# Norm of differential attention's outputs per tile with tokens in the partitions, their turn later and in banks 4 and 5, operand splits inside the last eight tiles' turns

## The reference, cut to what matters

```python
def diff_attention(q, k_sh, v_sh, ...):           # 6 heads of 2 x 64, values 128 wide
    ...
    p = jax.nn.softmax(s, axis=-1)
    attn = (p[:, :, 0] - lam * p[:, :, 1]).astype(v.dtype)
    o = jnp.einsum('bhqk,bkhe->bqhe', attn, v)    # allowed keys end with the query's chunk
    ...
    o = rms_norm_2(o, subln) * (1.0 - lam_init)   # over the 128 values of one head and token
    return o.reshape(B, S, BR_W)

y_mem = memory_cross_attention(q_mem, mem_n, w_mem_kv[l])
y = jnp.concatenate([y_br * jax.nn.silu(gate), y_mem * jax.nn.silu(g_mem)], axis=-1) @ w_out[l]
x = x + rms_norm_2(y, post_norm[l])
```

## Time and profile before

| | us |
|---|---|
| median of 3 runs | 3361.38 (3348.8 to 3362.89) |
| the profiled execution | 3360.08 |
| its span, first to last instruction | 3358.8 |
| stretch of the 48 attention tiles | about 2889 to 3176.4 |
| norm and first splits, no product running | 3176.4 to 3208.4 |
| products with `w_out` | 3208.4 to 3329 |
| last norm, residual and stores | 3329 to 3358.8 |

### The profile page before, as it was taken

One profiled execution on the slowest core, in us unless ns is written; L12 is line 12 of the kernel. 1 busy time (PEld: TensorE's weight loads), 2 busy tenths in 40 slices (PEclk: granted clock), 3 DMA queues, 4 the chain that ended last, 5 costly groups with the idle time before them and its releaser, 6 DMA issues. The chain is left out here.

```text
span 3358.8 us, 49940 instructions
## 1 busy us (share of the span) xinstructions
PE 2869.6 (85%) x20746; PEld 2299.7 (68%) x20746; DVE 1713.3 (51%) x3034; ACT 988.9 (29%) x1803; POOL 688.4 (20%) x531
## 2 busy tenths in 40 slices
PE   7978878799999999689999867777758899998767
PEld 6766666588888888467788546666637678766545
DVE  3425555544444444675554167676644433467534
ACT  3214444311111111633221211121134222244543
POOL 2112233211101110252111022222112211122123
PEclk9988999899999999899999979899979899999978
DMA  3111032011111111122112100000022201010222
GB/s 105 45 50 39 14 101 69 25 57 44 51 50 44 44 57 45 38 79 84 38 39 66 46 1 3 3 3 3 23 93 82 94 20 51 27 38 29 83 77 76
DMA packets 196449, 162.45 MB, mean 48 GB/s; under 512 B 5200, under 2 KB 173818, under 8 KB 195458
## 3 DMA queue, kind: packets, MB, share of 16 engines
q1 hardware_dynamic: 196226, 159.26, 15.1%
HBM read 137.19 MB, written 22.05 MB: 47 GB/s over the span
## 5 line engine op out<-in xcount | busy, mean ns | idle before, releaser
L721 PE MATMUL ps<-r,r 128*128 128x512 f32 (+1 forms) x2304 | 944.0, 410 | 142.4 <-DVE r L686 115.4
L722 PE MATMUL ps<-r,r 128*128 128x512 f32 (+1 forms) x2304 | 914.5, 397 | 0.0
L723 PE MATMUL ps<-r,r 128*128 128x512 f32 (+1 forms) x2304 | 912.8, 396 | 0.0
L721 PEld LDWEIGHTS ps<-r,r 128*128 128x128 f32 x2304 | 446.4, 194 | 274.2 <-DVE r L686 128.9
L667 POOL TENSOR_TENSOR sb<-sb 128x1024 f32<-128x1024 f32 x138 | 280.6, 2039 | 1350.3 <-DMA sb<-in_w_ffn_up 488.6
L723 PEld LDWEIGHTS ps<-r,r 128*128 128x128 f32 x2304 | 445.4, 193 | 95.3
L722 PEld LDWEIGHTS ps<-r,r 128*128 128x128 f32 x2304 | 446.3, 194 | 92.3 <-issue 6.2
L2234 PE MATMUL ps<-sb 64*64 64x64 f32 (+2 forms) x8832 | 298.2, 225 | 122.3 <-DVE sb L2485 29.5
L2234 PEld LDWEIGHTS ps<-sb 64*64 64x64 f32 (+1 forms) x8832 | 277.3, 135 | 151.3 <-issue 99.3
L686 DVE TENSOR_TENSOR r<-sb,r 128x1024 fp32r<-128x1024 f32 x198 | 274.2, 1392 | 192.1 <-ACT r L681 191.7
L681 ACT CAST r<-sb 128x1024 fp32r<-128x1024 f32 x198 | 204.9, 1044 | 228.3 <-POOL sb L667 228.2
(11 more groups left out here) (276 smaller groups left out, 3604.8 us busy)
## 6 DMA issues: line engine op xcount, KB each, us to landing
sb<-in_w_out SPq DMA_DIRECT2D x36, 512.0 KB, 4.1
sb<-in_a_w_in SPq DMA_DIRECT2D x29, 512.0 KB, 4.0
sb<-in_w_ffn_gate SPq DMA_DIRECT2D x22, 512.0 KB, 3.9
sb<-in_w_ffn_up SPq DMA_DIRECT2D x22, 512.0 KB, 3.9
sb<-in_w_ffn_down SPq DMA_DIRECT2D x22, 512.0 KB, 3.4
sb<-in_w_in SPq DMA_DIRECT2D x17, 512.0 KB, 4.0
sb<-in_x SPq DMA_DIRECT2D x16, 512.0 KB, 5.5
xs<-sb SPq DMA_DIRECT2D x4, 2048.0 KB, 9.5
```

The lines of the kernel that those rows point to most:

```text
L721: pe.matmul(self.out, w.hi[:, q, self.cols], hi, start=(q == 0), stop=False)
L722: pe.matmul(self.out, w.hi[:, q, self.cols], lo, start=False, stop=False)
L723: ins = pe.matmul(self.out, w.lo[:, q, self.cols], hi, start=False, stop=(q == w.nk - 1))
```

## The change

1. The norm moves into the attention. A new step `NormOut` t-1 stands behind `Scores` t+1. With the tokens in the partitions, a row's 128 values lie along one partition, so ACT squares them and sums them up in one instruction, then takes Ln and Exp of one column, and DVE multiplies the 128x128 tile by that column (L1942). `SubNorm` goes, with its matmuls, its table loads and the `Join` ahead of it.
2. `TurnOut` t-1 moves from between places 0 and 1 to behind `Exponentials` t+1, and its transpose goes into bank 4 or 5, as a group in the row of the probabilities' groups. Its ACT copy multiplies by the gain.
3. The gate is made as z / (1 + exp(-z)): Exp on ACT, a sum on POOL, a reciprocal of 128x512 on DVE (L1055), a product on POOL. The first two are placed at place 0 of the tile after the product's last, the other two at place 0 of the tile behind that.
4. The units are spread as 5, 5, 4, 4, 3, 2, 2, 1 over each of pairs 1 to 4 and 5, 4, 4, 4, 3, 2, 2 over pair 5; t = 39 to 47 get none. In a tile with more than 3 units, place 0 takes a third of what is due, rounded up, place 1 half of the rest and place 2 the remainder; a tile with fewer uses places 1 and 2.
5. The gates are fetched by two DMAs of 2 MB at t = 41. The multiplications, roundings and low parts (now all on POOL) of 15 of the 16 half tiles stand at place 3 of t = 42 to 46, and `Prepare` at t = 46. The 16th stands behind the first `w_out` product. The two DMAs that bring x back stand there too.

```diff
@@ class Attention, steps
             if t < last:
                 out += part(Scores, t + 1)
+            if t:
+                out += part(NormOut, t - 1)
             out += fill(t, 0)
-            if t:
+            if t and not self.diff:
                 out += part(TurnOut, t - 1)
...
             if t < last:
                 out += part(Exponentials, t + 1)
+            if t and self.diff:
+                out += part(TurnOut, t - 1)
             out += fill(t, 3)
@@ class NormOut
+            act.wait_ge(*s.scaled_out.at((of.id, i, iq)))
+            act.activation(of.junk, of.on[:, iq % 2, :], ACT.Square, accum_out=s4[:, 0:1]).then_inc(*s.out_squared.up((of.id, i, iq)))
+            act.wait_ge(*s.out_squared.at((of.id, i, iq)))
+            k.functions(act, LN_EXP_SET)
+            act.activation(s4[:, 1:2], s4[:, 0:1], ACT.Ln, bias=k.eps, scale=1.0 / P).then_inc(*s.out_ln.up((of.id, i, iq)))
+            act.wait_ge(*s.out_ln.at((of.id, i, iq)))
+            act.activation(s4[:, 1:2], s4[:, 1:2], ACT.Exp, scale=-0.5).then_inc(*s.out_rstd.up((of.id, i, iq)))
...
+            dve.wait_ge(*s.out_rstd.at((of.id, i, iq)))
+            dve.tensor_scalar(o, o, s4[:, 1:2], None, ALU.mult).then_inc(*s.out_normed.up((of.id, i, iq)))
@@ class EvictGate
-        act.activation(self.gated, self.buf(st), ACT.Tanh).then_inc(*s.stage_tanh.up(st.id))
+        act.activation(self.gated, self.buf(st), ACT.Exp, scale=-1.0).then_inc(*s.stage_exp.up(st.id))
...
+        pool.tensor_scalar(self.gated, self.gated, 1.0, None, ALU.add).then_inc(*s.stage_sum.up(st.id))
+
+    def inverse(self, dve, st):
+        s = self.s
+        dve.wait_ge(*s.stage_sum.at(st.id))
+        dve.reciprocal(self.gated, self.gated).then_inc(*s.stage_inverse.up(st.id))
@@ layer_b
+    for st, t in spread(k, put, prods, 0, [5, 5, 4, 4, 3, 2, 2, 1] * 4 + [5, 4, 4, 4, 3, 2, 2], True):
+        put(t + 1, 0, GateExp(k, st))
+        put(t + 2, 0, GateProduct(k, st))
...
+    put(last - 6, 0, *fetch)
+    order = [(j, h) for h in range(2) for j in (6, 7, 0, 1, 2, 3, 4)]
+    for n, (j, h) in enumerate(order):
+        put(last - 5 + n * 5 // len(order), 3, his[h][j], los[h][j])
+    put(last - 1, 3, his[0][5], los[0][5])
+    put(last - 1, 3, Prepare(k))
...
-    yield from finish_layer(k, 1, stored, SubNorm(k, q, lam.e[0], F))
```

More of the change, by code:

```diff
@@ L1864, in act @@
         act.wait_ge(*s.turned_out.at((of.id, i, iq)))
[L1865 removed]
+        act.activation(of.out(i, iq), src, ACT.Copy, scale=k.sub if of.diff else 1.0).then_inc(*s.out_copied.up((of.id, i, iq)))
 class ForgetBiasRows:
@@ L3096, in finish_layer @@
     yield from weave(first, (1, back[:1]), *by(3, splits[1], 1), (6, back[1:]))
[L3097 to L3106 removed]
+    yield from chain(k, ev, y, acc, second, back=[st.event() for st in back])
 def layer_b(k):
@@ new lines, in layer_b @@
+    y, acc = k.at(F, KT, S), k.halves(F + 14336)
+    ev = EvictSquares(k, lambda i: y[:, i, :], acc, V["post_norm_2"][:, KT:2 * KT])
+    first, second = two_passes(k, lambda i: columns(k, A["w_out_2"][1], i * P), ev, op)
+    back = [Dma(k, k.x[:, :, span_of(h)], k.scratch["xs"][:, :, span_of(h)], f"dma_back{h}",
+                [k.keep[h].event(), *[("lo_of_x_pool", (keys[h], j)) for j in range(KT)]]) for h in range(2)]
+    norms = [Rsqrt(k, acc[h], acc[h], 4 + h, D, ev.summed(h)) for h in range(2)]
@@ new lines, in layer_b @@
+    adds = [residual(k, h, y=y, r=acc[h], rstd_id=norms[h].id) for h in range(2)]
+    rows = k.at(F + 8192, 4, D)
+    store = [Store(k, i, rows, [("x_added", (adds[i // 4][0].key, KT - 1))] if i % 4 == 0 else []) for i in range(ST)]
+    there = [After(k, pool=[st.event()]) for st in back]
+    yield from weave(first, (1, [back[0], his[1][5], los[1][5], back[1]]))
+    yield from weave(second, (1, [norms[0], there[0]]), *by(2, adds[0], 2), (6, store[:2]), (7, store[2:4]))
+    yield from [norms[1], there[1], *adds[1], *store[4:]]
@@ new lines, in spread @@
+def spread(k, put, prods, begin, counts, act_later):
+    left, due, ends = [(st, q) for st in prods for q in range(st.units())], 0, []
+    for n, count in enumerate(counts):
+        due += count
+        for place, share in ((0, 3), (1, 2), (2, 1)) if count > 3 else ((1, 2), (2, 1)):
+            units = []
+            while left and len(units) < -(-due // share) and (not units or units[0][0] is left[0][0]):
+                units.append(left.pop(0))
+            due -= len(units)
+            if units:
+                st = units[0][0]
+                put(begin + n, place, Part(k, st, [q for _, q in units], act_later))
+                if units[-1][1] == st.units() - 1:
+                    ends.append((st, begin + n))
+    assert not left, len(left)
+    return ends
```

203 lines of the change are left out of this document (103 added, 100 removed).

## The result

The changed kernel takes 3396.43 us (median of 4, 3393.95 to 3403.09), the kernel before on the same chip 3357.15: a ratio of 1.0114, 95% interval 1.0093 to 1.0136. It is slower by about 39 us, where 20 us less were forecast, and it lies above the stated range of 3313 to 3368. The profiled execution has a span of 3396.3 us.

A forecast was written before the change was run, and what follows sets the result against it. The prediction took PE to bound the filled attention pairs. Its terms, -52.3 (end), -18 (pairs 1 to 5), +39 (new waits there) and +11 (pair 6), gave -20 from 3360.1: 3340 us, range 3313 to 3368.

The forecast's parts named there:

- The end, -52.3: From the last ScaleOut to the third w_out product: 16.3 us instead of 68.6, so -52.3 us.
- What then bounds a filled pair is PE: Pairs 1 to 5: PE takes 43.0 us a pair against 46.8, the chain being covered; -18 us.
- Reciprocal, 15 x 1.1 = +17: Pairs 1 to 5: 15 gate reciprocals of 2.7 us each, partly hidden beside PE's units, cost 17 us.
- Shared gate buffer and Exps, +6 and +5: Pairs 1 to 5: +6 for Exps waiting where products end in neighbouring tiles, +5 for more casts and Exps on ACT.
- Bank 7, +11: Pairs 1 to 5: evictions of products ending at places 0 or 1 hold the next product's unit; +11 us.
- Pair 6, +11: t = 39 to 46, without units: 54.5 us instead of 43.8, so +11 us.
- the bare chain: Pair 6: the chain through DVE and ACT alone, without units, taken as 36 us.
- the last gates with the wait for their transfer: Pair 6: the last gate's reciprocal, 2.4 us, and a DVE stop of 5 us for the gates' fetch.
- Rival 3: Attention pairs: DVE becomes the bound, slower; break-even at a reciprocal of 4.1 us, 3380 and more at 5.5; chance 0.09.
- Rival 2: Gate reciprocals on the chain scale more steeply, 4.3 us each, 22 us more in all: 3362; chance 0.13.
- Rivals 1 and 4: 1: reciprocals and evictions hidden, 3306 to 3325 (0.22); 4: end not coming forward, a third of 52 stays, 3357 (0.08).
- the signs of right and of wrong: For the reciprocal L1055: 2.5 to 2.9 us would show right, near 0.7 or above 4 wrong.

The follow-up runs named there:

- e5: e2 together with e3's unit layout, every product ending at place 2: 3324.71 us, ratio 0.9886.
- e12: Kernel before with the gate alone changed to exp, ln and exp on ACT and the product on GpSimd: 3359.63 us, ratio 0.9996.
- e14: Changed kernel with GpSimd's gate product a turn later, beside the maxima; where ends neighbour, the second's exp, sum and reciprocal move too: 3383.15 us.
- e2: Changed kernel with the gate as exp, ln, exp on ACT, without reciprocal or GpSimd's sum: 3336.09 us, ratio 0.9940.
- e13: Changed kernel with GpSimd's gate product made of one column instead of 512: 3385.55 us, ratio 1.0089.
- e3: Changed kernel with units laid out as before for four pairs (ends at place 2), four a tile in the fifth: 3366.49 us, ratio 1.0025.
- e6: e2 with the 15 splits behind the attention's last turn and the weight's preparation in the last tile's turn: 3338.69 us, ratio 0.9927.
- e8: e2 with only the next weight's preparation moved from t = 46 to the last tile's turn: 3336.49 us, ratio 0.9924.
- e16: Changed kernel with the gate's reciprocal made of 256 of its 512 columns: 3374.53 us, ratio 1.0039.
- e10: e11 with only the first half's eight splits in the tiles, the rest between the first w_out pass's products: 3309.88 us, ratio 0.9847.
- e11: Changed kernel with gate on ACT, ends at place 2, splits spread over t = 42 to 47, weight's preparation in the last tile: 3315.80 us.
- e4: Kernel before with only the changed kernel's gate (exp, sum, reciprocal, product): 3411.12 us, ratio 1.0152.

## Why the prediction was wrong, point by point

The step that failed is the one on pairs 1 to 5: PE was taken as what bounds them, with the chain through DVE and ACT covered and a good part of each reciprocal hidden beside PE's units. The runs showed that length in the chain is covered for the smaller part only: t = 1 to 38 lost 75.7 us where 21 were forecast, and the change came out 39 us slower although the end gained what was forecast.

- **The end, -52.3.** Right: 183.1 to 127.5 us behind the last ScaleOut, -55.6. The first product started 1.94 us behind it (forecast 1.75), the third 16.6 (16.3), 52.0 us less than before; the other 3.6 us come after that, where the prediction had no change.
- **"What then bounds a filled pair is PE", -18.** The step that failed first. 43.0 us a pair was a sum of PE's busy time with no gap in it. (Of its 43.9 us, 5.7 lie in 2943 to 2949, where the granted clock is 0.50, so 2.9 come off for the clock and not 2.3; the sum would be 42.4.) With the same units as before, late turn and norm, e5 needs 178.3 us for 31 tiles, 46.0 for eight, where e12 needs 183.3. PE is busy for 166.2 of the 178.3, so it waits 3.1 us in eight tiles. The gain of the late turn is 5 us there and 1 us over t = 1 to 38 against the kernel before, since e5's fifth pair takes more units. The chain through DVE and ACT is not covered by PE's work; the earlier trace rows showed a unit between turn and transposes, and taking it out of the chain doesn't bring the tile down to PE's own sum. Which of the waits that are left hold PE was not tried one by one.
- **Reciprocal, 15 x 1.1 = +17.** Two terms of it were off. Its length: 3.345 us, not 2.7. The slope between one and 16 columns is 4.5 ns, that between 256 and 512 is 6.2 ns a column. That line gives 0.25 us for 16 columns, where 0.229 were measured; why the small rows lie off it isn't shown. The prediction's estimate of 4.3 us, worked out from the repeat count in the Trainium skill, "VectorE: DVE Perf Modes", section "Walkthrough: the 8-slice pipeline in each mode", does not agree with the trace either; the measurement lies between. And its cover: 1.6 us of each were to lie beside PE's units. With collisions and shared buffer mostly taken out it costs (276.1 - 240.4) / 15 = 2.4 us each (e14 against e2), +36, so some 0.9 us of each are covered. The 2.4 hold what e2 changes besides, GpSimd's sum left out and the Exps moved; 12.9 us of the 36 show as longer waits of PE for evictions (29.5 against 16.6).
- **Shared gate buffer and Exps, +6 and +5, and what was missing.** From e14 to the changed kernel are 22.1 us: up to 11.3 are the collision of GpSimd's product with the combination (e13), which had no term in the sum for pairs 1 to 5, and about 11, by the trace only, go with ACT's two stops of 6.0 us, at t = 11 and 26 as the prediction placed them.
- **Bank 7, +11.** Right mechanism, too small: 18.9 us (e2 against e5), with 16.6 us of waits.
- Together t = 1 to 38: -1 + 18.9 + 35.7 + 22.1 = +75.7, where +21 were forecast. The sum closes by itself, since each term is the step from one run to the next, and another order of the steps gives other terms: 36.1 for the layout with the reciprocals in place (e3), then 40.6 for reciprocals and collisions (e3 against e5). Against the forecast the largest misses are the reciprocal (19), PE as the bound (17) and the collision (11).
- **Pair 6, +11.** Measured +17.5. The term that failed is the bare chain, taken as 36 us and 1.5 for the clock: with neither units nor splits nor weight (e6) the pair takes 42.5, with PE's clock granted at 0.76 of full speed. How much of the 5.0 us more is the clock isn't shown. The weight ahead of the combination costs 6.4 (e8; forecast 3.5; 1.7 of it came back in the last tile there), the splits 7.3 (e6 against e8; forecast 6), the last gates with the wait for their transfer 5.1 (forecast 7.4). 42.5 + 6.4 + 7.3 + 5.1 = 61.3. The tile behind it, 4.0 us before and 5.5 after, had no term.
- **The rivals.** Rival 3 had the outcome right, slower, and at a length for which the prediction still saw a gain (it broke even only at 4.1 us). Its mechanism came true in part: DVE's length is the largest cost, but DVE isn't full, busy for 224 of 298 us and idle for 52 while ACT's exponentials run. Its sum for each further microsecond, 14 us, was about right (e16: 17, collisions included); what it started from was not. Rival 2, a steeper slope, is half true: 3.345 us, between the 2.7 taken and its 4.3. Rivals 1 and 4 are out: the reciprocals were not hidden, and the end came forward.
- **The signs.** The stops of ACT at t = 11 and 26 (6.0 us each) and DVE's wait for the gates' DMA at t = 42 (4.2 us, forecast 5) came. L1055 at 3.3 us fell between the signs of right and of wrong, and the clock of pair 6 is 0.73.

## What to carry to other kernels

In this loop three engines hand one tile round, and DVE, idle for 30% of the time, had little room for a long operation: of 3.3 us ahead of the hand-over up to 2.4 showed in the time, and more with what the operation released. So measure one such operation before counting on gaps. Put the work on the engine whose wait lies behind its own hand-over (here two ACT passes instead of one DVE reciprocal and a GpSimd sum: some 58 us by the ratios), and look at what the finished operation releases, because that runs beside the next critical step. Moving work forward out of an idle stretch paid here only as far as the first consumer needs it: half the splits beat all of them (e10 against e11).

## What the runs showed of the hardware

- DVE's reciprocal of 128x512 f32 takes 3.345 us (3343 to 3348 ns over 16), 256 columns 1.746, 6.2 ns a column; a multiply of 512 columns takes 0.63.
- A DVE operation with two SBUF inputs stands still while a GpSimd operation that began before it runs: 0.22 became 1.24 us, 1.15 became 2.75, for a step of one column as for 896 (e4). The norm's multiply of 128x128, with one SBUF tile, does so too: 0.28 became 1.73 (e2). The maxima, which read PSUM and SBUF (0.68 and 0.69 us beside GpSimd), and the one-column reciprocals kept their length.
- A sigmoid as exp, ln(1 + x), exp on ACT takes 0.62, 0.72 and 0.63 us for 512 columns and the trace of e2 has no table load in t = 1 to 38, where the norm takes ln and exp too.
